# A two-block network on one core: FFN and projection entries fed with x times norm weight, the token scale applied where PSUM is read; memory norms and the expert scatter in other places

## What is computed

```python
def rms_norm(x, g):
    y = xf * lax.rsqrt(jnp.mean(xf * xf, axis=-1, keepdims=True) + EPS)
    return (y * g.astype(jnp.float32)).astype(x.dtype)
def swiglu(h, w13, w2):
    gate, up = jnp.split(h @ w13, 2, axis=-1)
    return (jax.nn.silu(gate) * up) @ w2
# first network, layer 0 (short convolution) and 1 (latent attention)
x = x + FFN_HALF * swiglu(rms_norm(x, norm_g[layer, 0]), ffn_w13[layer, 0], ffn_w2[layer, 0])
h = rms_norm(x, norm_g[layer, 1])          # h @ w_in: gate_b, gate_c, xt, q_mem
y = gate_b * causal_short_conv(gate_c * xt, conv_w)
k, v = jnp.split(rms_norm(mem, mem_norm_g) @ w_mem_kv, 2, axis=-1)
x = x + jnp.concatenate([y_mix, y_mem], axis=-1) @ w_out[layer]
x = x + FFN_HALF * swiglu(rms_norm(x, norm_g[layer, 2]), ffn_w13[layer, 1], ffn_w2[layer, 1])
```

## Time and profile before

| | |
|---|---|
| runs, median of 3 | 3653.23 us (3649.91 to 3656.42) |
| the profiled execution, own time | 3658.82 us |
| its span | 3657.0 us |
| PE busy | 3339.3 us, 91% |
| DVE, ACT, POOL busy | 1723.2, 1607.0, 1231.2 us |
| mean granted clock | 0.953 |

### The profile page before, as it was taken

One profiled execution on the slowest core, in us unless ns is written; L12 is line 12 of the kernel. 1 busy time (PEld: TensorE's weight loads), 2 busy tenths in 40 slices (PEclk: granted clock), 3 DMA queues, 4 the chain that ended last, 5 costly groups with the idle time before them and its releaser, 6 DMA issues.

```text
span 3657.0 us, 51781 instructions
## 1 busy us (share of the span) xinstructions
PE 3339.3 (91%) x20194; PEld 2976.5 (81%) x20194; DVE 1723.2 (47%) x1948; ACT 1607.0 (44%) x1869; POOL 1231.2 (34%) x507
## 2 busy tenths in 40 slices
PE   6988898698588998999899989998999999999998
PEld 5987897598458988898799988887777777877776
DVE  4223302412432017234222172342888888888887
ACT  2333342233123324433133234340667666766765
POOL 3864484287007826323288353240000000000000
PEclk8998999899789999999999999998999999999999
DMA  4542353254114443333354433244789888988986
GB/s 159 181 153 104 140 182 127 92 183 162 46 58 151 182 150 133 122 136 130 139 184 184 150 134 120 104 151 149 299 314 352 325 314 325 357 307 316 352 317 254
DMA packets 97077, 707.30 MB, mean 193 GB/s; under 512 B 10784, under 2 KB 10784, under 8 KB 10944
## 3 DMA queue, kind: packets, MB, share of 16 engines
q1 hardware_dynamic: 96624, 703.37, 51.5%
q10 hardware_dynamic: 288, 2.10, 0.2%
q0 software_dynamic: 48, 0.13, 0.0%
HBM read 704.51 MB, written 1.05 MB: 193 GB/s over the span
## 4 chain that ended last, share of the span: by engine, by line
PE 83%; DVE 10%; ACT 3%; DMA 2%; issue 2%; POOL 0%; DVEq 0%; SPq 0%; ACTq 0%
PE bank L525 20%; PE bank L526 19%; PE bank L527 19%; PE bank L560 10%; DMA ring<-experts 2%; PE bank L557 2%; DVE kept L1443 2%; PE bank L831 2%; DVE rs L1440 1%; PE bank L598 1%; DVE kept L1539 1%; PE bank L957 1%; PE bank L678 1%; PE bank L656 1%; PE bank L574 1%
## 5 line engine op out<-in xcount | busy, mean ns | idle before, releaser
L488 POOL TENSOR_TENSOR half_lo<-ring,half_hi 128x1024 fp32r<-128x1024 f32 x502 | 1230.3, 2460 | 1209.5 <-ACT half_hi L1068 1209.4
L525 PE MATMUL bank<-h_hi,half_hi 128*128 128x256 f32 x3088 | 891.8, 289 | 92.7 <-DVE h_lo L1453 79.3
L526 PE MATMUL bank<-h_lo,half_hi 128*128 128x256 f32 x3088 | 884.5, 286 | 0.0
L527 PE MATMUL bank<-h_hi,half_lo 128*128 128x256 f32 x3088 | 883.8, 286 | 0.0
L1068 ACT ACTIVATE half_hi<-ring 128x1024 fp32r<-128x1024 f32 x502 | 528.5, 1056 | 694.9 <-PE bank L527 621.4
L1384 ACT ACTIVATE expert_parts<-ring 128x1024 fp32r<-128x1024 f32 x672 | 674.3, 1053 | 317.4 <-DMA ring<-experts 263.5
L525 PEld LDWEIGHTS bank<-h_hi,half_hi 128*128 128x128 f32 x3088 | 604.5, 196 | 100.8 <-DVE h_lo L1453 82.1
L526 PEld LDWEIGHTS bank<-h_lo,half_hi 128*128 128x128 f32 x3088 | 604.2, 196 | 0.4
L527 PEld LDWEIGHTS bank<-h_hi,half_lo 128*128 128x128 f32 x3088 | 603.5, 195 | 0.0
L1882 DVE TENSOR_TENSOR expert_parts<-ring,expert_parts 128x1024 fp32r<-128x1024 f32 x448 | 527.7, 1221 | 85.3 <-ACT expert_parts L1384 83.4
L1465 DVE TENSOR_TENSOR hid<-sg,bank 128x512 f32<-128x512 f32 x58 | 39.9, 687 | 776.8 <-PE bank L527 776.8
(11 more groups left out here) (266 smaller groups left out, 4075.4 us busy)
## 6 DMA issues: line engine op xcount, KB each, us to landing
ring<-experts SPq DMA_DIRECT2D x336, 1024.0 KB, 4.8
ring<-stream SPq DMA_DIRECT2D x330, 1024.0 KB, 4.8
lent<-mem ACTq DMA_DIRECT2D x2, 1024.0 KB, 4.8
con<-consts SPq DMA_DIRECT2D x1, 1473.0 KB, 8.4
kept<-mem SPq DMA_DIRECT2D x1, 1024.0 KB, 5.0
kept<-x_in SPq DMA_DIRECT2D x1, 1024.0 KB, 14.4
out<-kept SPq DMA_DIRECT2D x1, 1024.0 KB, 3.9
par<-params SPq DMA_DIRECT2D x1, 317.5 KB, 8.7
```

Of the source, the lines that this page charges most:

```text
L488: nc.gpsimd.tensor_tensor(half_lo[:, h % HALVES, :], ring[:, u % RING, s * HALF:(s + 1) * HALF], half_hi[:, h % HALVES, :].bitcast(F32), A ...
L525: mm(dst, w_hi, x_hi, start=start, stop=False, skip_group_check=shared)
L526: mm(dst, w_hi, x_lo, start=False, stop=False, skip_group_check=shared)
L527: return mm(dst, w_lo, x_hi, start=False, stop=stop, skip_group_check=shared)
```

## The change

1. At the seven entries `opening` takes the place of `x_norm_split` on PE. ACT writes `h_hi` straight from X times g (`x_high`, 8 copies with a scale), and DVE writes `h_lo` from X, g and `h_hi` (`x_low`, 8 instructions). PE does the two matmuls with `h_hi` for up to three halves, then those with `h_lo`, then the sum of squares, then the fourth half. After out0, out1 and the second network's wo, three of the four pairs of tiles are made while the projection still runs.
2. The token's scale `rs_x` is applied where PSUM is read. In `hidden`, DVE now has five instructions for three: gate times scale, up times scale, silu(gate) times up, the high part, the rest. Silu is read from that scaled copy (`gate_scaled`), and stands one unit later on ACT. In conv_in and mla_in the copies out of PSUM become products with `rs_x`, or with its square for gate_c.
3. The norm of the memory goes into the first FFN (layer 0) and into ffn01 (layer 1), as `beside` work of DVE behind the first `hidden` steps. `memkv0` stands behind conv_in's first unit, and `memkv1` where it was, without the norm ahead of it. The rotation angles go from the start to behind `hidden(2)` of ffn00, and the lambda terms behind `hidden(0)` of ffn01.
4. conv_in's units 4 to 9 stand in the memory attention, one or two beside each head, and the convolution is cut in three parts.
5. The scatter of pass n-1 stands in pass n, behind its fourth unit; the first pass scatters zeros, and one scatter follows the last pass.
6. At the start x, constants and parameters are loaded first, then three units, then the memory.

The diff, cut to its core:

```diff
@@ order of the stream, loads at the start
+        if name == "conv_in":
+            out += [(name, 0, 1), ("memkv0", 0, 2), (name, 1, n - 1)]
...
-            sp.dma_start(mem_raw, mem1).then_inc(loaded, 16)
+            sp.dma_start(X, x_in).then_inc(x_loaded, 16)
...
+            sp.dma_start(mem_raw, mem1).then_inc(mem_in, 16)
@@ PE
+            def opening(first, second=None):
+
+                n = t.add("entry", 1)
+                parts = [first + (0,), first + (1,)] + ([second + (0,)] if second else [])
+                for i, (b, u, m) in enumerate(parts):
+                    w_hi, w_lo = half(u, m)
+                    for k in range(KT):
+                        if i == 0 and k % 2 == 0:
+                            pe.wait_ge(xg_hi, 4 * n - 4 + k // 2 + 1)
...
+                        mm(dst, w_hi[:, cols], h_hi[:, k, :], start=k == 0 and m == 0, stop=False, skip_group_check=True)
+                        mm(dst, w_lo[:, cols], h_hi[:, k, :], start=False, stop=False, skip_group_check=True)
+                for i, (b, u, m) in enumerate(parts):
...
+                            pe.wait_ge(xg_lo, 4 * n - 4 + k // 2 + 1)
+                        last = mm(b[:, m * 256:m * 256 + 256], w_hi[:, k * PARTS:(k + 1) * PARTS], h_lo[:, k, :],
+                                  start=False, stop=k == KT - 1, skip_group_check=True)
+                    last.then_inc(first_done if m == 0 else unit_done, 1)
+                x_sums()
+                if second:
+                    column_half(*second, 1)
...
-                gate_up(0, u0)
+                opening((bank[pair[0][0]], u0), (bank[pair[0][1]], u0 + 1))
+                if beside:
+                    beside()
+
+                wait(pe, rs_ready, t.now("rs"))
...
-            mem_kv(0)
-            x_norm_split()
-            ffn(START["ffn00"], D_FF // 256)
-            x_norm_split()
+            ffn(AT["ffn00"][0], D_FF // 256, lambda: norm(KT, KT, ones))
+            project_opening(conv[0:1])
+            wait_normed()
+            project(mem_n[0], memkv[0:1])
             norm(2, 1, C("blocks"))
+            project(mem_n[0], memkv[1:2], token_major=True)
+            norm(2, 1, C("blocks"))
+            project(None, conv[1:4])
             wait_normed()
+            mem_attention(lambda h: project(None, (conv[5:6], conv[7:8], conv[8:9], conv[9:10])[h]),
+                          lambda h: project(None, conv[6:7] if h == 0 else []),
+                          lambda: project(None, conv[4:5]))
...
                 columns(2, bank[1])
-                pe.wait_ge(moe_x, 4 * n + 4)
+                scatter(n)
+                pe.wait_ge(moe_x, 4 * n + 8)
                 columns(4, bank[2])
@@ ACT
+            def x_high(g, j):
+                wait(act, x_ready, 4 * t.now("x") - 4 + j + 1)
+                for k in (2 * j, 2 * j + 1):
+                    last = nc.scalar.activation(h_hi[:, k, :], X[:, k, :], ACT.Copy, scale=g(k))
+                last.then_inc(xg_hi, 1)
...
                 def silu(i, r=0):
-                    nc.scalar.activation(sg[:, i % 2, :], bank[2 * (i % 2)][:, :], ACT.Silu).then_inc(sg_ready, 1)
+                    act.wait_ge(gate_scaled, 2 * r + (h0 + i + 1))
+                    nc.scalar.activation(sg[:, i % 2, :], sg[:, i % 2, :], ACT.Silu).then_inc(sg_ready, 1)
...
+                        step(u0, 3 * i, r, lambda: silu(i, r))
@@ DVE
+            def x_low(g, j):
+                dve.wait_ge(xg_hi, 4 * t.now("entry") + j + 1)
+                for k in (2 * j, 2 * j + 1):
+                    last = v.scalar_tensor_tensor(h_lo[:, k, :], X[:, k, :], g(k), h_hi[:, k, :].bitcast(F32),
+                                                  ALU.mult, ALU.subtract)
...
                 def hidden(i, odd):
-                    v.tensor_tensor(hid[:, odd, :], sg[:, odd, :], bank[2 * odd + 1][:, :], ALU.mult).then_inc(hid_step, 1)
+                    dve.wait_ge(unit_done, ffn_unit(u0, i) + 1)
+                    v.tensor_tensor(sg[:, odd, :].rearrange("p (m t) -> p m t", m=2), two(bank[pair[odd][0]]), both(rs_x),
+                                    ALU.mult).then_inc(gate_scaled, 1)
+                    dve.wait_ge(unit_done, ffn_unit(u0, i) + 2)
+                    v.tensor_tensor(hid[:, odd, :].rearrange("p (m t) -> p m t", m=2), two(bank[pair[odd][1]]), both(rs_x),
+                                    ALU.mult).then_inc(hid_step, 1)
+                    v.tensor_tensor(hid[:, odd, :], sg[:, odd, :], hid[:, odd, :], ALU.mult).then_inc(hid_step, 1)
...
+                    if type(i) is int and i < len(beside):
+                        beside[i]()
...
+            ffn(AT["ffn00"][0], D_FF // 256, 0.5, (mem_first, lambda: mem_part(0, range(4, 8)), angles, lam_start))
+            ffn(AT["ffn01"][0], D_FF // 256, 0.5, (lam_end, lambda: mem_part(1, range(0, 4)), lambda: mem_part(1, range(4, 8))))
...
                 low(1)
+                low(2)
+                taken(n)
+                low(3)
+                low(4)
+                scattered(n)
```

More of the change, by code:

```diff
@@ L1125, in ffn @@
+                if then:
+                    then()
                 chunk(1)
@@ new lines, in mem_root @@
+            def mem_root():
+                t.add("norm", 1)
+                act.wait_ge(ss_ready, t.add("rs", 1))
+                nc.scalar.activation(rs_m, bank[3][:, 0:TOK], ACT.Sqrt, bias=C("eps"), scale=1.0 / D).then_inc(rs_ready, 1)
+            opening(gain("norm_g", 0), AT["ffn00"][0])
+            ffn_x(AT["ffn00"][0], D_FF // 256, mem_squares, mem_root)
+            conv, memkv = AT["conv_in"], AT["memkv0"]
+            opening(gain("norm_g", 1), conv[0])
+            done(conv[0])
```

660 lines of the change are left out of this document (399 added, 261 removed).

## The result

The changed kernel takes 3530.12 us (median of 4 runs, 3518.30 to 3532.06), the kernel before 3652.86 in the same comparison: the ratio is 0.9658, with a 95% interval of 0.9645 to 0.9671. It is 123 us faster; 3521 was forecast, within 3498 to 3552. The profiled execution took 3530.66 us, its span is 3528.8. Between the two profiled executions lie 128.2 us, and it is these that the sum of 132.5 has to be held against.

A forecast was written before the change was run, and what follows sets the result against it. PE was busy for 91% of the span, so gains could come only where it stands still or runs slowly. Terms 33 + 3 + 44 + 32 + 9 - 4.5 + 16 = 132.5 us, off the median 3653.2, gave 3521 us, range 3498 to 3552.

The forecast's parts named there:

- Start: Kernel start to `gate_up(1)` of ffn00: PE begins near 17 us, `gate_up(1)` near 42 instead of 75.0; saves 33 us.
- Convolution layer: Last FFN result to first out0 matmul: 102 us instead of 105.5, with 10 of idle time; saves 3 us (-7 to +11).
- ffn01, ffn11, ffn2: Entries of these FFNs: three of four pairs made beside the projection, 15.6 us instead of 31.1 at ffn01; saves 44 us.
- ffn10: Entry of ffn10 with memkv1: memkv1 begins at once, then the split matmuls; saves 32 us (27 to 35) of 68.
- mla_in: Entry of mla_in: sum and first unit take 11 us, up to 13 with slow clock; saves 9 us (8 to 10).
- FFN steps: 58 FFN steps: `gate_up(i + 1)` covers the 7.5 us chain, but beside work stops PE; loses 4.5 us (0 to 12).
- Experts: Expert passes: 3.2 us saved per seam, seven times, less an extra scatter and memsets; net 16 us (8 to 24).
- A: Rival: the expert seam gives nothing, as DMA and DVE have little slack; 3543 us, chance 0.12.
- D: Rival: slower than before, as the lengthened chain of `hidden` exceeds its cover in every step; 3695 us, chance 0.03.
- C: Rival: entries still wait, for third-half low parts or bank 3, 6 us at each of seven; 3563 us, chance 0.05.
- B: Rival: DVE and POOL exclude each other in convolution and beside work, 15 and 12 us more; 3548 us, chance 0.13.
- L1469's successor still near 2.9: Sign: the successor of a 512-column DVE instruction with two SBUF inputs still takes about 2.9 us, PE never waiting in a running FFN.

The follow-up runs named there:

- experiment 10: Changed kernel with hidden chain in PSUM, beside work spread over more steps, convolution taps read from PSUM, first third behind head 0's probabilities: 3502.96 us, ratio 0.9586.
- experiment 1: Changed kernel, but the up half is scaled, multiplied by silu and split in place in its PSUM bank: 3505.63 us, ratio 0.9598.
- experiment 3: Changed kernel with the expert seam alone undone: scatter at a pass's end, no extra scatter or memsets, old order of low parts: 3544.45 us.
- 7: Changed kernel with one more unread 512-column DVE instruction of two SBUF inputs ahead of the low part in each of 58 FFN steps: 3535.14 us.
- experiments 2: Changed kernel with angles, lambda and memory products spread over more FFN steps, and the mixers' logarithm instructions left out: 3514.45 us.
- experiment 9: Changed kernel with 40 filler matmuls of constants in PE's idle time between mla_in and its attention: 3516.76 us, ratio 0.9625.
- experiment 12: experiment 10's kernel with 40 filler matmuls in mla_in's stage, 24 ahead of the wait for x's norm and 8 ahead of c_kv's: 3507.01 us.

## Why the prediction was right, and where it was not

It was right as a whole: 128.2 us between the profiled executions against a sum of 132.5, or 3530 measured against 3521. (The terms' bounds, taken as independent, give 3507 to 3538 and not 3535; the stated range is not touched.) Point by point:

- **Start**: 35.7 instead of 33. PE began at 17.1 us, silu at 36.8, `gate_up(1)` at 39.3. Half clock lasted only to 21.9 us, and the root needed 1.4 us of PE's waiting.
- **Convolution layer**: 4.4 instead of 3. Idle time at the turns was 6.3 us, not 10. The mechanism named, thirds of the convolution held by POOL, is there (four taps took 3.87 us in head 1 and 1.80 in head 2), but it was not what PE waited for: with it gone the waits fell by 0.5 us only (experiment 10). Most of them are for the scaling of the probabilities, held by POOL too, which I had not counted.
- **ffn01, ffn11, ffn2**: 16.0 + 14.9 + 14.3 = 45.2 instead of 44. **ffn10**: 31.4 instead of 32. Both as worked out, with 15.1 us where 15.6 were forecast.
- **mla_in**: 9 forecast, 0.0 in the stage. The failing step is "after, 1.6 + 5.8 + 3.7 = 11 ... Saved: 9 us": right for the entry (8.9), but taken to reach the end. Behind it PE works between stops, at half clock for 109 us in the changed kernel and for 89 in the one before, and how long decides over 10 us. The clock was charged in the forecast only where PE stands at the entry itself.
- **FFN steps**: -4.5 forecast (0 to -12), -22.2 measured, outside the bounds. Two steps failed. "`gate_up(i + 1)`, 11.5 us, covers it" is true for 53 of 58 steps; for the last of each FFN there is no `gate_up`, only a `down` of 5.8, so 1.7 us of wait and 0.7 of restart and clock were paid five times, 12 us (experiment 1 took the waits away, and the three bodies without a lump became 2.0 us shorter each). And the two lumps cost some 6.3 and 3.8 us (the bodies of ffn00 and ffn01 less 2.4) instead of 3 and 1.5: I charged the stop, not the half clock behind it, and took lambda's 16-column instructions as short, where each may wait out one of POOL's.
- **Experts**: 16 forecast, 28.9 measured. Only 24.1 of them are the seam (experiment 3). The term "3.2 per seam" is 4.1: waits fall by 3.1 and not 2.6, and what is left for the clock around the stop is 1.0 and not 0.6. The extra scatter costs 3.8 + 0.9, as forecast, the memsets 2.2 instead of 1.5. The other 5 us are the two long passes of before (135.7 and 135.5). Since long passes turn up in one profiled execution or another, with the old seam or the new, they seem to belong to the execution and not to the change; they also fit the profiled execution's being 5.6 us above its median. What makes a pass long was not tried.

That the total came out near is in part luck: -18 and -9 against +13 for the experts, +3 for the mixers and +7 for all the rest; and 5 of the 13 come from the execution that was profiled. Without these the sum of 132.5 stands against 123, which is also the difference of the medians. Of the rivals, A is refuted by experiment 3, D by 7; C did not occur (4.9 us at five entries, instead of 6 at each of seven). B's mechanism occurred in the beside work, in the chain and in the heads, but not at B's price: the convolution layer became 4.4 us shorter.

What the list of signs said: first product near 17, no wait for a low part at an entry (2.0 us for a high part is the longest), 15.1 instead of 16 for ffn01, 3.5 us at the angles with the releasing chain as named, all seen. In the heads the stops were 2.7, 1.9 and 1.2 us where 2 to 6 were named, and from pass to pass there are 4 us less where 3 were. "L1469's successor still near 2.9" was not: it takes 0.76, and its two predecessors 2.2 and 2.4.

## What to carry to other kernels

For work that hides a chain, look at the last round of a loop by itself: the cover that all others have is missing there. Before pricing a DVE instruction beside a busy GpSimd engine, look where its operands are, and put one in PSUM where the chain matters. And when an edit's time is off by less than some 10 us in a kernel with idle PE stages, compare stage by stage before believing it: unchanged stages moved by up to 10 us here.

## What the runs showed that I had not expected

- The granted clock of one and the same stage took different courses in different kernels: 194.1 us at 0.72 and 183.5 to 186.5 at 0.76 to 0.79, with PE busy for 143 or 131 to 135 us for 538 matmuls. The changed kernel stayed in the long course in both its profiles, and so did experiments 2 and 3. With matmuls of constants in PE's idle times it took 181.2 (experiment 9) and the stage of the latent keys from 83.5 to 80.3 (experiment 12). The Trainium skill ("TensorE: Matmul & The Clock Gate", "HAM oscillation — how this bites in real kernels") describes waits that let the clock fall again each round. The trace agrees that waits and half clock go together, but here the clock did not rise between the waits at all, 0.50 from 882 to 974 us. What selects between the courses for equal instructions stays open.
- DVE scales and multiplies in place in a PSUM bank in 0.70 us for 512 columns, no slower than into SBUF (0.69).
- An extra instruction in a chain beside POOL can be nearly free: every second one slips into the gap between two of POOL's (0.69 instead of 2.5).
